# adaLN's column vectors by a multiply-and-sum along the row, in a hybrid decoder layer on one core

## What is computed

```python
ada = jax.nn.silu(c) @ w_ada[l] + b_ada[l]
sh1, sc1, gt1, sh2, sc2, gt2 = jnp.split(ada[:, None, :], 6, axis=-1)
h = x * (1.0 + sc1) + sh1
proj = h @ w_in[l]
...
x = layer_norm(DEEPNORM_ALPHA * x + gt1 * (mixed @ w_out[l]), ln1_g[l], ln1_b[l])
h2 = x * (1.0 + sc2) + sh2
y = peer(h2, peer_wq[l], peer_subkeys[l], peer_u[l], peer_v[l])
x = layer_norm(DEEPNORM_ALPHA * x + gt2 * y, ln2_g[l], ln2_b[l])
```

## Time and profile before

| | us |
|---|---|
| median of 3 runs | 1025.08 (1023.74 to 1026.29) |
| the profiled execution | 1024.66 |
| its span | 1022.9 |
| TensorE busy with matmuls | 1008.0 (99%) |
| VectorE busy | 778.5 (76%) |
| ScalarE busy | 513.8 (50%) |
| GpSimd busy | 322.5 (32%) |

### The profile page before, as it was taken

How to read it: one execution, slowest core, us unless ns; L and a number is a source line. 1 busy time by engine, 2 the same in 40 slices (tenths; PEclk the granted TensorE clock), 3 DMA queues, 4 the chain that set the end, 5 groups by cost and what they waited for, 6 DMA issues and landing times.

```text
span 1022.9 us, 18122 instructions
## 1 busy us (share of the span) xinstructions
PE 1008.0 (99%) x6925; PEld 933.3 (91%) x6925; DVE 778.5 (76%) x1592; ACT 513.8 (50%) x756; POOL 322.5 (32%) x206
## 2 busy tenths in 40 slices
PE   8999999999999999999999999999999999999996
PEld 8999889999999999999999999988888888888785
DVE  7978888874898698886677788766666866776666
ACT  5785646545444544445444434454554545545443
POOL 1001000011887478777788867000010000000002
PEclk9999999999999999999999999999999999999998
DMA  9889858776555577777666666567779778887651
GB/s 354 357 271 377 298 181 296 261 229 210 174 177 177 155 205 188 183 184 188 166 146 145 154 157 145 182 213 221 216 235 324 237 235 260 263 280 217 220 189 43
DMA packets 96855, 222.82 MB, mean 218 GB/s; under 512 B 27520, under 2 KB 45952, under 8 KB 96000
## 3 DMA queue, kind: packets, MB, share of 16 engines
q1 hardware_dynamic: 74336, 207.93, 61.9%
q0 software_dynamic: 22144, 13.71, 8.8%
q10 hardware_dynamic: 288, 0.01, 0.0%
HBM read 211.06 MB, written 10.55 MB: 217 GB/s over the span
## 4 chain that ended last, share of the span: by engine, by line
PE 93%; DVE 2%; DMA 2%; ACT 1%; POOL 0%; issue 0%; POOLq 0%; SPq 0%; ACTq 0%; DVEq 0%
PE px L1171 33%; PE pw L863 17%; PE pw L864 17%; PE pw L865 16%; PE px L1147 3%; DMA ada<-in_ada 2%; PE px L1116 1%; PE pv L864 1%; PE pv L863 1%; PE pv L865 1%; PE px L863 0%; DVE w_lo L1225 0%; PE px L864 0%; PE px L865 0%; PE px L1040 0%
## 5 line engine op out<-in xcount | busy, mean ns | idle before, releaser
L568 ACT ACTIVATE w_hi<-raw 128x1024 fp32r<-128x1024 f32 x312 | 328.7, 1057 | 320.3 <-PE px L1171 159.0
L1225 DVE TENSOR_TENSOR w_lo<-raw,w_hi 128x1024 fp32r<-128x1024 f32 x285 | 347.4, 1226 | 140.9 <-ACT w_hi L568 138.4
L863 PE MATMUL pw<-a_hi,w_hi 128*128 128x256 f32 x1280 | 367.2, 287 | 0.3 <-DVE a_lo L1492 0.3
L865 PE MATMUL pw<-a_hi,w_lo 128*128 128x256 f32 x1280 | 362.6, 283 | 0.0
L864 PE MATMUL pw<-a_lo,w_hi 128*128 128x256 f32 x1280 | 362.5, 283 | 0.0
L541 POOL DMA_INDIRECT gates_spill<-gate,place x128 | 228.0, 1781 | 83.3 <-issue 47.5
L863 PEld LDWEIGHTS pw<-a_hi,w_hi 128*128 128x128 f32 x1280 | 245.7, 192 | 1.9 <-issue 1.2
L864 PEld LDWEIGHTS pw<-a_lo,w_hi 128*128 128x128 f32 x1280 | 245.8, 192 | 0.1
L865 PEld LDWEIGHTS pw<-a_hi,w_lo 128*128 128x128 f32 x1280 | 245.7, 192 | 0.0
L1171 PE MATMUL px<-w_hi,ws_hi 128*128 128x512 f32 x512 | 159.1, 390 | 0.0
L1171 PE MATMUL px<-w_hi,ws_lo 128*128 128x512 f32 x512 | 158.6, 389 | 0.0
(11 more groups left out here) (350 smaller groups left out, 1166.5 us busy)
## 6 DMA issues: line engine op xcount, KB each, us to landing
raw<-in_u SPq DMA_DIRECT2D x128, 512.0 KB, 4.1
raw<-in_v SPq DMA_DIRECT2D x128, 512.0 KB, 4.7
raw<-in_ws SPq DMA_DIRECT2D x56, 512.0 KB, 6.5
ada<-in_w_ada SPq DMA_DIRECT2D x32, 512.0 KB, 7.0
gates_spill<-zero POOLq DMA_DIRECT2D x16, 512.0 KB, 7.3
g_row<-gates_spill SPq DMA_DIRECT2D x128, 64.0 KB, 4.4
ada<-in_ada SPq DMA_DIRECT2D x6, 1024.0 KB, 11.0
raw<-in_w SPq DMA_DIRECT2D x7, 768.0 KB, 10.9
```

The costliest lines, as they stand in the source:

```text
L568: return nc.scalar.activation(out, in_, ACT.Copy, **kw)
L863: nc.tensor.matmul(out, lh, rh, start=start and x == 0, stop=False)
L865: last = nc.tensor.matmul(out, ll, rh, start=False, stop=stop and x == len(pairs) - 1)
L1225: v.tensor_tensor(w_lo[:, m % RING], raw[:, m % RING], w_hi[:, m % RING].bitcast(F32), ALU.subtract).then_inc(lo_ready, 1)
```

## The change

The weights of the four column vectors are laid out on the host with the output column on the partition and the 1024 inputs along the row. silu(c) is brought onto every partition as a row, `sc_row`: eight float32 matmuls with `sc_col` broadcast and the identity, then two copies on ScalarE. Each 128 columns of a vector are then one multiply-and-sum on VectorE (`tensor_tensor_reduce`), which adds the bias as its start value in the first part. `part`, `mod1` on TensorE, ScalarE's two products and its bias copies go; so do the matmuls of lines 1064 and 1073. gate1 keeps its sum over partitions. Two blocks of the first part (HGRN2's i) are now made for 512 columns at once, one matmul of 512 in place of two of 256. The first chunk's halves are split in another order, and the warm-up is 6 + 20 matmuls and not 27 + 10.

```diff
+        sc_row = sb("sc_row", AR + 26624, [D])
...
             for c in range(KC):
                 act.wait_ge(x_chunk_landed[c], 16)
-                act.wait_ge(mod1_done, c + 1)
-                for s in range(2 * c, 2 * c + 2):
-                    last = nc.scalar.activation(mod1[:, s:s + 1], px[0][:, s:s + 1], ACT.Identity, bias=b_cols[:, s:s + 1])
...
+                act.wait_ge(mod1_ready, c + 1)
...
                 if c + 1 < KC:
                     split_hi1(c + 1)
-                if c + 2 < KC:
-                    products(c + 2)
...
+            def first_rows(t, c):
+
+                q, w = slice(t * P, (t + 1) * P), slice(256 * HI, FW)
+                last = three(p1[HI + t][:, :], [(a_hi[:, c, q], a_lo[:, c, q], hi1[c % 2][:, w], lo1[c % 2][:, w])],
+                             start=c == 0, stop=c == KC - 1)
...
-            pe.wait_ge(consts, 1)
-            keep(27, px[3])
-            mod1(0)
-            keep(10, px[3])
+            pe.wait_ge(consts, 2)
+            keep(6, px[3])
+            pe.wait_ge(sc_ready, 1)
+            for k in range(KC):
+                last = nc.tensor.matmul((pw[0], px[0])[k // 4][:, (k % 4) * P:(k % 4 + 1) * P],
+                                        sc_col[:, k:k + 1].broadcast_to([P, P]), ident[:, :], start=True, stop=True)
...
+            keep(20, px[3])
...
-                if b == WOUT:
-                    for c in range(KC):
-                        last = nc.tensor.matmul(px[2][:, KC + c:KC + c + 1], acc[:, 1, c * P:(c + 1) * P],
-                                                ones_col[:, :], start=True, stop=True)
-                    last.then_inc(mod2_done, 1)
...
-                    if b == WOUT and h == 1:
-                        pe.wait_ge(ya_copied, HEADS // 2)
-                        for c in range(KC):
-                            nc.tensor.matmul(px[2][:, c:c + 1], acc[:, 0, ADA_W + c * P:ADA_W + (c + 1) * P],
-                                             ones_col[:, :], start=True, stop=True)
...
+                w = ada[:, t % ADA_SLOTS]
+                if t >= KC:
+                    c, s = divmod(t - KC, 2)
+                    x = s * KC + c
+                    ins = v.tensor_tensor_reduce(w, w, sc_row[:, :], 1.0, 0.0, ALU.mult, ALU.add, mod2_sum[:, x:x + 1])
...
+            def modulation(c):
+
+                w = ada1[c % CHUNK_SLOTS]
+                dve.wait_ge(ada1_landed[c % CHUNK_SLOTS], 16 * (c // CHUNK_SLOTS + 1))
+                for s in range(2):
...
+                    x = 2 * c + s
+                    ins = v.tensor_tensor_reduce(w[:, s], w[:, s], sc_row[:, :], 1.0, b_cols[:, x:x + 1], ALU.mult, ALU.add,
+                                                 mod1[:, x:x + 1])
+                ins.then_inc(mod1_ready, 1)
...
-            pool.wait_ge(mod2_done, 1)
             pool.wait_ge(gt1_done, 1)
```

More of the change, by code:

```diff
@@ L169, in layer @@
         lo1 = [sb(f"lo1_{s}", AR + (6144, 32768)[s], [FW], F32R) for s in range(2)]
-        ada1 = [sb(f"ada1_{s}", AR + (0, 8192, 19456)[s], [KC, 2 * P]) for s in range(CHUNK_SLOTS)]
-        part = [sb(f"part{s}", AR + 31232 + 512 * s, [2, 2 * P]) for s in range(2)]
+        ada1 = [sb(f"ada1_{s}", AR + (0, 8192, 19456)[s], [2, D]) for s in range(CHUNK_SLOTS)]
         lf = sb("lf", AR + 0, [HG * T])
@@ L602, in split_hi1 @@
                 copy(hi1[c % 2][:, :], raw1[c % CHUNK_SLOTS][:, :]).then_inc(hi1_ready, 1)
-            def products(c):
-                s = c % CHUNK_SLOTS
-                act.wait_ge(ada1_landed[s], 16 * (c // CHUNK_SLOTS + 1))
-                act.wait_ge(mod1_done, c - 1)
-                for k in range(2):
-                    last = nc.scalar.activation(part[c % 2][:, k], ada1[s][:, k], ACT.Identity, scale=sc_col[:, k:k + 1])
-                last.then_inc(prod_ready, 1)
-            split_hi1(0)
-            act.wait_ge(b_cols_ready, 1)
+            for half in range(2):
+                act.wait_ge(sc_row_done, half + 1)
+                copy(sc_row[:, half * 512:(half + 1) * 512], (pw[0], px[0])[half][:, :]).then_inc(sc_row_ready, 1)
+            act.wait_ge(raw1_landed[0], 16)
+            copy(hi1[0][:, 0:FW // 2], raw1[0][:, 0:FW // 2]).then_inc(hi1_ready, 1)
             for c in range(KC):
                 act.wait_ge(x_chunk_landed[c], 16)
-                act.wait_ge(mod1_done, c + 1)
-                for s in range(2 * c, 2 * c + 2):
-                    last = nc.scalar.activation(mod1[:, s:s + 1], px[0][:, s:s + 1], ACT.Identity, bias=b_cols[:, s:s + 1])
-                last.then_inc(mod1_copied, 1)
-                act.wait_ge(mod1_copied, c + 1)
+                act.wait_ge(mod1_ready, c + 1)
                 for out in (a_hi, xT):
@@ L937, in transposes_x1 @@
                 last.then_inc(x1T_done, 1)
-            def mod1(c):
-                pe.wait_ge(part_ready, c + 1)
-                for s in range(2):
-                    last = nc.tensor.matmul(px[0][:, 2 * c + s:2 * c + s + 1], part[c % 2][:, 0, s * P:(s + 1) * P],
-                                            ones_col[:, :], start=True, stop=True)
-                last.then_inc(mod1_done, 1)
             def first_block(b, c):
@@ L951, in first_block @@
                     q = slice(s * P, (s + 1) * P)
-                    pair = (a_hi[:, c, q], a_lo[:, c, q], hi, lo) if b in NATURAL else (hi[:, q], lo[:, q], a_hi[:, c], a_lo[:, c])
-                    last = three(p1[b][:, s * T:(s + 1) * T], [pair], start=c == 0 and s == 0, stop=c == KC - 1 and s == 1)
+                    last = three(p1[b][:, s * T:(s + 1) * T], [(hi[:, q], lo[:, q], a_hi[:, c], a_lo[:, c])],
+                                 start=c == 0 and s == 0, stop=c == KC - 1 and s == 1)
                 if c == KC - 1:
@@ L1058, in after @@
                     for half in range(2):
-                        last = nc.tensor.matmul(px[half][:, :], ones_pp[:, :], acc[:, 0, half * 512:(half + 1) * 512],
+                        last = nc.tensor.matmul(px[half][:, :], ones_pp[:, :], acc[:, half * 512:(half + 1) * 512],
                                                 start=True, stop=True)
                     last.then_inc(gt1_done, 1)
-                if b == WOUT:
-                    for c in range(KC):
-                        last = nc.tensor.matmul(px[2][:, KC + c:KC + c + 1], acc[:, 1, c * P:(c + 1) * P],
-                                                ones_col[:, :], start=True, stop=True)
-                    last.then_inc(mod2_done, 1)
             for b in range(FIRST, NA):
@@ L1298, in _ @@
             v.tensor_scalar(om_lb[:, :], lb_col[:, :], -1.0, 1.0, ALU.mult, ALU.add)
-            early, late = range(4), range(4, KC)
-            sum_part(0, early)
             dve.wait_ge(small_landed, 16)
```

139 lines of the change are left out of this document (54 added, 85 removed).

## The result

The changed kernel takes **1019.17 us** (median of 5 runs, 1019.0 to 1019.83), the kernel before in the same session 1024.93 us (median of 5, 1023.74 to 1026.29). The ratio is 0.9944 with a 95% interval of 0.9933 to 0.9956: 5.8 us faster, where 4.9 were forecast, and inside the forecast range.

The account below looks back on a forecast made before the run. TensorE was taken as the bound, waiting in the first part for VectorE, with DMA close behind. Gains 2.46 + 0.14 + 2.3 = 4.9 us turn 1025.08 into 1020.2; 8-in-10 range 1018.5 to 1023.3, forecast's own 1018.5 to 1021.7.

Parts of the forecast that it names:

- The bound that takes over: First part: VectorE's chunk falls from 4.96 to 4.73 us, so the weights' landing, 4.80 us a chunk, becomes the bound.
- the three signs of being wrong: Pair over 3 us; weights landing later than one chunk in 4.8 us; new TensorE idle between 55 and 230 us.
- The pair: VectorE's two multiply-and-sums over 1,024 columns per first-part chunk: 2 x (1.26 + 0.10) = 2.72 us, reads included.
- The first part was mis-sized: First-part gain: 2.46 us from an earlier last chunk plus 0.14 from its shorter TensorE work, 2.6; range 1.8 to 3.3.
- chunk 2's weights land at 20.45 as before: First part: this landing stays unchanged, TensorE follows at 24.3 instead of 25.90, and five chunks of 4.80 reach 48.3.
- The start: Before chunk 2: the pair starts after 8.6 us, TensorE starts at 13.0, chunk 1 at 19.2 after 2 us idle.
- The later sums: Around w_out's first block: 3.40 us of single-column matmuls go, a 1.1 us m_lo wait appears; 2.3 stay (2.0 to 3.4).
- VectorE's cover: Later sums: VectorE's 14.4 us idle between 100 and 200 us hides the added pass time; without it, up to 2.3 lost.
- (1): Rival: accumulator read drains VectorE's pipe, pair 3.2 us, first part brings only 0.4; 1022.4 us; chance 0.10.
- (2): Rival: head start lost behind, the DMA-paced stage from 60 to 100 us swallows the 2.6; 1022.8 us; chance 0.08.
- (3): Rival: TensorE's clock falls in the 2 us gap before chunk 1, some 3.7 of the gain go; 1023.9 us; chance 0.05.
- (4): Rival: VectorE's row sum runs at the scan's pace, pair 4.96 us, result +17, 1042 us; chance 0.09.

Follow-up runs that it names:

- dose256: Changed kernel with one extra multiply-and-sum over 256 columns on VectorE in each of chunks 2 to 7 of the first part; 1019.50 us.
- dose1024: Changed kernel with one extra multiply-and-sum over 1,024 columns on VectorE in each of chunks 2 to 7 of the first part; 1023.69 us.
- light: Changed kernel with half of adaLN's weights of chunks 3 to 7 not loaded, 2.6 MB in all; 1016.88 us.
- light_before: Kernel before the change with half of adaLN's weights of chunks 3 to 7 not loaded; 1023.90 us.
- cols256: Changed kernel with the first part's two 512-column blocks cut back into matmuls of 256 columns; 1019.63 us.
- old_sums: Changed kernel with the later column sums as before, including 16 single-column matmuls on TensorE; only the first part is new; 1021.76 us.
- late12: Changed kernel with 12 matmuls, not 6, ahead of the wait for the last m_lo in w_out's first block; 1018.03 us.
- hold: Changed kernel with the next two blocks' four loads held back on SyncE until chunk 6's weights have landed; 1019.10 us.

## Why the prediction was right

**The bound that takes over.** The central step was that VectorE's chunk would drop just below the landing of the weights and that the landing would then set the pace. It did: high halves waiting for the DMA in every chunk from chunk 1 on, a spacing of 4.76 and, with the longer last interval, 4.83 on average from 24.50 to 43.83, for 4.80 forecast from bytes and the earlier trace rows. dose256, dose1024 and light show it by intervention. Of the three signs of being wrong, one (weights later than one chunk in 4.8 us) was touched by this 0.03, without a consequence.

**Where the first part's gain lies.** It is not where the forecast put a third of it. Of 2.46 us, 1.60 were to come at chunk 2 (24.3 for 25.90) and 0.86 from the five faster chunks behind. Measured, TensorE is 3.04 ahead at chunk 2 and only 3.17 at the last chunk: the early landing of chunk 2 is followed by one 5.40 us later (24.50), so the closer spacing shows only from chunk 3 on, where the lead grows from 2.61 to 3.17.

The 3.04 are 1.35 by the earlier landing and 1.69 by a shorter chain from the landing to a_lo (25.33 - 20.45 = 4.88 before, 22.29 - 19.10 = 3.19 after). About half of that chain's gain, 0.84, is ScalarE's wait for adaLN's next weights, which light_before shows; the rest is about the price of the two products that VectorE had behind the low half (0.90 in the earlier trace rows). The prediction counted the new chain rightly (3.85 us to TensorE, measured 3.76). What it read wrongly is the old one: it has ScalarE waiting for weights until 20.45 and never in the way, but ScalarE waits for adaLN's weights twice more, at 22.96 and 27.76, and the first of these waits holds up chunk 2. It also gave TensorE's own chunk as 4.96, which is the spacing; without the idle time it is 4.8.

**The pair.** Taken at 2.72, it is 2.41. The reduction of the earlier trace rows was the right row to go by, and the 0.10 for each read was too much: the read takes 0.08, beside the next pass, and a pass with it 1.21. It made no difference, since VectorE's chunk of 4.43 (4.73 forecast) lies below the landing either way. The scan's price, 4.96 for the pair, was far off. The Trainium skill's rule that the prediction names, by which two float32 sources from SBUF halve the pace, is stated for the scalar-tensor-tensor form; the multiply-and-sum, another instruction in the trace, reads just such sources and isn't slowed either, at 1.28 us for 1,024 columns.

**The first part was mis-sized: 3.2 us for 2.6.** The failing term is "chunk 2's weights land at 20.45 as before". They landed at 19.10. The load is issued at nearly the same time in both kernels (6.66 and 6.78 us), with the same bytes in front. In the kernels with the new first part, which are alike up to there, it lands anywhere from 18.9 to 20.0 us, while chunk 3's weights land at 24.4 to 24.9 in all but light (in the changed kernel 24.50, by the forecast 25.25). The error of 1.35 at chunk 2 had become 0.62 at chunk 7: 43.83 where 20.45 + 5 x 4.80 gives 44.45. By issue and landing, the forecast 44.45 fits the kernel before itself, whose last chunk's weights are issued at 34.47 and there at 44.3, hidden behind VectorE; in the changed kernel the weights land some 0.5 us earlier from chunk 3 on (24.5 for 25.1), and in the nine other kernels with the new first part and all its loads the last chunk's come at 43.5 to 44.0. The other pieces are small: landing to TensorE 3.76 for 3.85; the last chunk 4.34 long for 4.24, a gain of 0.04 and not 0.14, of which cols256 gives the wider matmuls 0.05. The lesson in the working: one landing in one execution is a poor anchor, since it scatters by a microsecond where the sum over several chunks does so by half of that. That the measured time lay so near the forecast owes something to this: 0.6 us more in the first part and 0.4 more in the sums against 0.4 lost behind. Whether the old first part has its weights later by the edit or by scatter (chunk 2's at 20.45 and, in light_before, 20.01, but in light 19.99 with the new one) was not tried.

**The start** went as said, a little faster: first pass at 7.85 (8.6), TensorE's chunk 0 at 12.14 (13.0), chunk 1 at 18.12 after 1.49 us of idleness (19.2 and 2), with a granted clock of 1.00, the 2.4 GHz level, in this stretch and behind it.

**The later sums: 2.66 us for 2.3.** The mechanism was right and old_sums isolates it. The wait for m_lo, forecast at 1.1, left a hole of 1.03; 3.40 - 1.03 = 2.37, and 2.46 was measured from gate1's sums to LN1. The other 0.2 lies between the first part and gate1, where every trace with the old sums needs 143.37 to 143.39 us and every one with the new 143.16 to 143.20. It is one step: there TensorE's first matmul of a block comes 0.26 us behind the one before, with the new sums 0.12, and the next 0.19 in place of 0.12. The block waits for VectorE's br_b, and two of the later passes stand ahead of it (old_sums, then the changed kernel):

```profile
184.12 2.67 DVE L1233 SCALAR_TENSOR_TENSOR acc<-ada,sc_col,acc 128x1024 f32<-128x1024 f32 x2
186.72 0.69 DVE L1314 TENSOR_TENSOR br_a<-pw,sig_a 128x512 f32<-128x512 f32 x1
188.45 0.69 DVE L1407 TENSOR_TENSOR br_b<-pv,sig_b 128x512 f32<-128x512 f32 x1
189.28 0.36 PE L850 MATMUL pw<-y_hi,w_hi 128*128 128x256 f32 x1
```

```profile
184.34 1.22 DVE L1211 CUSTOM_DVE_ANT_0 ada<-ada,sc_row 128x1024 f32<-128x1024 f32 x1
186.63 0.68 DVE L1297 TENSOR_TENSOR br_a<-pw,sig_a 128x512 f32<-128x512 f32 x1
```

Two old passes take 2.60 us to br_a, two new ones 2.29. So the later multiply-and-sum, counted by the prediction at 1.36 in place of 1.28, is the cheaper one here: 1.15 us against 1.30 from start to start. VectorE's cover held: 85.22 us busy between 100 and 200 where it was 85.56.

**What was not foreseen: 0.4 us go back behind.** The lead is 5.86 at the start of table v and 5.45 near the end; the spans differ by 5.5 and the medians by 5.8, a difference that the scatter of the executions covers. TensorE's list of waits in the changed kernel has one row more in this stretch:

```profile
PE px L1148 <- DVE ws_lo L1651: 0.3, 1, 0.3
```

VectorE stands there in front of the gates' rows. Both kernels have that wait (the first row is of before, the second of the changed kernel), and my reading, which no run tests, is that TensorE notices when enough rows arrive late one after the other:

```profile
772.70 0.29 DVE L1684 TENSOR_TENSOR W<-W,g_row 128x128 f32<-128x128 f32 x1 [3.61 <-DMA g_row<-gates_spill]
```

```profile
766.65 0.29 DVE L1644 TENSOR_TENSOR W<-W,g_row 128x128 f32<-128x128 f32 x1 [3.23 <-DMA g_row<-gates_spill]
```

Seven of the thirteen traces have the row, at 0.2 to 0.7 us, light_before among them, and six don't. The row alone doesn't measure the loss: between the same two marks (start of table v, gate2's sums) late12 takes 0.01 us more than before, but old_sums and cols256, without the row, 0.30 and 0.42, and hold and light_before, with it, 0.87 and 1.06; old_sums and cols256 have a hole of 0.26 and 0.24 in front of a matmul with ws_hi (at 775.45 and 773.29) to which no wait is put down. It follows neither the edit nor the length of the lead, so I count it as scatter of these loads; no run was made to settle it.

**The rivals.** (1) The read drains nothing: the next pass starts with it. (2) The head start is not lost: 3.21 at 52 us and 3.41 at 195. ScalarE does still wait for weights in the second part, 3.57 us at 87.34 where it was 4.24, with no wait of TensorE behind it. (3) The clock stayed at 1.00. (4) The sum along the row does not run at the scan's pace; how far a long pair would have led, dose1024 shows for the first part: its gain is used up before 3.56 us.

## What to carry to other kernels

When a column vector is built by scaling and adding rows and then summing over partitions, storing the weights with the output column on the partition makes it one multiply-and-sum per 128 columns with no matmul behind, and the price here is that of a plain elementwise pass. Look also at what leaves the chain from a landing to the first matmul: of the first part's 3.2 us, 1.7 came from there, half of it a wait of ScalarE for the next chunk's weights. Before counting the gain of a shortened engine, work out the next bound from the bytes: here the landing let through at most 0.20 of the 0.53 us a chunk that VectorE gave up (4.96 to 4.76, not to 4.43), and 0.14 on average from chunk 3 on. And where a load is the bound, look at the time from its landing to the first matmul: ordering the products so that those with the high halves come first took 1.7 us more off the same first part.

## What the chip showed that I had not expected

- The accumulator's read behind a multiply-and-sum (0.08 us) costs no time of its own: the next pass has the same start, 38.76. A pass over 1,024 columns moves the next by 1.21 us in the first part and by 1.15 in the later sums and in dose1024; one over 256 by 0.35.
- Loads issued behind a load did not slow it: with 2 MB more in the queue or without, the weights landed at 43.83 and 43.98 us, some 11 us after their issue; issued 2.04 us later (dose1024), they were there at 43.8 as well.
- The landing of a load in a full queue scatters by up to 1.1 us between executions (chunk 2 at 18.9 to 19.2 or 19.7 to 20.0 with the new first part), and a chunk later 0.5 us of it is left (24.4 to 24.9).
